# A three-branch mixer layer with a seven-product output projection: other halves of K, sums made earlier, a block-wise finish

## The reference, cut to what matters

```python
h = _rmsnorm(x, norm_g)                    # x: 1024 x 2048
proj = einsum('sd,de->se', h, w_in)        # to 5120 columns
ua, va, ga, q, k, v, gb, xc, gc = split(proj)
ya = _spatial_gating(ua, va, ...)          # mixer A, 4 tiles of 128 columns
yb = _swa_sink_attention(q, k, v, ...)     # mixer B, 8 tiles
yc = _multiscale_pool(xc, ...)             # mixer C, 4 tiles
mix = concatenate([ya * silu(ga), yb * silu(gb), yc * silu(gc)])
out = _rmsnorm(x + einsum('se,ed->sd', mix, w_out), final_g)
```

## Time and profile before

| what | value |
|---|---|
| time, median of 3 runs | 1334.62 us (1334.57 to 1339.37) |
| the profiled execution: time / span | 1337.06 us / 1335.3 us |
| TensorE matmul busy | 1277.5 us (96%) |
| VectorE / ScalarE busy | 798.5 us (60%) / 456.7 us (34%) |
| mean granted TensorE clock | 0.985 |
| DMA, mean over the span | 177 GB/s, 235.99 MB |

### The profile page before, as it was taken

How to read it: one execution, slowest core, us unless ns; L and a number is a source line. 1 busy time by engine, 2 the same in 40 slices (tenths; PEclk the granted TensorE clock), 3 DMA queues, 4 the chain that set the end, 5 groups by cost and what they waited for, 6 DMA issues and landing times. The chain is left out here.

```text
span 1335.3 us, 15960 instructions
## 1 busy us (share of the span) xinstructions
PE 1277.5 (96%) x6374; PEld 1058.6 (79%) x6374; DVE 798.5 (60%) x1157; ACT 456.7 (34%) x661; POOL 45.1 (3%) x38
## 2 busy tenths in 40 slices
PE   6999999999999998999999999999794999999995
PEld 4988888888888887888888888888673888888884
DVE  7444787767345564535786765357573665545664
ACT  6433433333232344424333333233322212223135
POOL 4200000000000212000000000000000000000000
PEclk9999999999999999999999999999898999999998
DMA  6642221212266444323121222357888689867857
GB/s 214 199 126 97 93 95 64 95 64 95 66 236 231 161 165 153 113 85 111 68 95 64 95 67 92 106 210 279 335 325 320 252 309 384 328 229 255 326 200 267
DMA packets 67514, 235.99 MB, mean 177 GB/s; under 512 B 7249, under 2 KB 10353, under 8 KB 54257
## 3 DMA queue, kind: packets, MB, share of 16 engines
q1 hardware_dynamic: 67440, 234.99, 49.4%
HBM read 192.23 MB, written 42.73 MB: 176 GB/s over the span
## 5 line engine op out<-in xcount | busy, mean ns | idle before, releaser
L1304 PE MATMUL t_bank<-op_hi,w_hi 128*128 128x512 f32 x1088 | 432.0, 397 | 22.7 <-DVE op_lo L902 10.8
L1305 PE MATMUL t_bank<-op_lo,w_hi 128*128 128x512 f32 x1088 | 426.6, 392 | 0.0
L1306 PE MATMUL t_bank<-op_hi,w_lo 128*128 128x512 f32 x1088 | 426.4, 392 | 0.0
L897 DVE TENSOR_TENSOR w_lo<-raw,w_hi 128x1024 fp32r<-128x1024 f32 (+1 forms) x172 | 203.0, 1220 | 320.4 <-ACT w_hi L678 320.4
L678 ACT ACTIVATE w_hi<-raw 128x1024 fp32r<-128x1024 f32 (+1 forms) x172 | 169.4, 1031 | 376.6 <-PE t_bank L1306 313.5
L1304 PEld LDWEIGHTS t_bank<-op_hi,w_hi 128*128 128x128 f32 x1088 | 206.0, 189 | 69.8 <-issue 14.8
L1305 PEld LDWEIGHTS t_bank<-op_lo,w_hi 128*128 128x128 f32 x1088 | 206.0, 189 | 43.0 <-issue 1.7
L1306 PEld LDWEIGHTS t_bank<-op_hi,w_lo 128*128 128x128 f32 x1088 | 205.6, 189 | 43.3
L1304 PE MATMUL n_bank<-w_hi,s_ring 128*128 128x512 f32 x448 | 176.0, 393 | 17.4 <-DVE y L986 17.4
L1306 PE MATMUL n_bank<-w_hi,s_ring 128*128 128x512 f32 x448 | 175.3, 391 | 0.0
L1305 PE MATMUL n_bank<-w_lo,s_ring 128*128 128x512 f32 x448 | 175.2, 391 | 0.0
(11 more groups left out here) (158 smaller groups left out, 1139.2 us busy)
## 6 DMA issues: line engine op xcount, KB each, us to landing
raw<-w_dram SPq DMA_DIRECT2D x78, 1024.0 KB, 4.9
s_ring<-s_parts SPq DMA_DIRECT2D x112, 512.0 KB, 5.6
s_parts<-stage SPq DMA_DIRECT2D x40, 256.0 KB, 3.1
s_parts<-stage SPq DMA_DIRECT2D x16, 512.0 KB, 3.6
raw<-w_o_dram SPq DMA_DIRECT2D x8, 1024.0 KB, 9.0
y_w<-w_o_dram SPq DMA_DIRECT2D x8, 1024.0 KB, 9.0
y<-x_dram SPq DMA_DIRECT2D x8, 1024.0 KB, 8.7
mix<-x_t_dram SPq DMA_DIRECT2D x20, 256.0 KB, 6.5
```

The lines of the kernel that those rows point to most:

```text
L897: ve.tensor_tensor(w_lo[:, J % 2, part], w_source(J)[:, part], w_hi[:, J % 2, part].bitcast(F32), ALU.subtract).then_inc(lo_done, 1)
L1304: pe.matmul(psum_out, stat[0], mov[0], start=first, stop=False)
L1305: pe.matmul(psum_out, stat[0], mov[1], start=False, stop=False)
L1306: return pe.matmul(psum_out, stat[1], mov[0], start=False, stop=last)
```

## The change

It pairs neighbouring mix tiles in the two halves of K (w_out's rows are reordered on the host to match), moves the sums, splits them in two steps a slot apart, keeps A22 in two stage slots of its own semaphore, changes the waits of load_s, swaps two residual loads, and runs the last product's add and the finish in one loop over the blocks. Cut to its core:

```diff
-SUM_ORDER = (0, 1, 2, 3) + tuple(4 + j for j in POOL_ORDER)
-SUM_AT = (70, 72, 73, 75, 76, 78, 80, 81)
-SUM_ITEMS = (Q_S3, Q_S1, Q_S2, Q_S4, Q_A22)
+K_1 = (0, 2, 4, 6, 8, 10, M_C + POOL_ORDER[0], M_C + POOL_ORDER[2])
+K_2 = (1, 3, 5, 7, 9, 11, M_C + POOL_ORDER[1], M_C + POOL_ORDER[3])
+SUM_AT = (56, 60, 64, 68, 71, 74, 77, 81)
...
             def load_first_half(r):
+                else:
+                    sp.wait_ge(s_saved[0], 32 * r)
+                    sp.wait_ge(s_saved[1], 32 * r)
+                if r == 4:
                     sp.wait_ge(o_ready, PIECES * HALVES)
...
+                sp.dma_start(a11, mix_first[K_1[r]]).then_inc(a_loaded, 16)
+                sp.dma_start(a12, mix_first[K_2[r]]).then_inc(a_loaded, 16)
...
+            def save_first_sums(r):
+                m1, m2 = sum_tiles(r)[2:4]
+                sp.wait_ge(s_lo_done, 5 * r + 1)
+                sp.dma_start(s_parts[Q_A22, r].rearrange("p h s -> p (h s)"),
+                             stage[:, 0:2, :].bitcast(F32).rearrange("p h s -> p (h s)")).then_inc(a22_saved, 16)
+                sp.wait_ge(s_lo_done, 5 * r + 2)
+                save_halves(Q_S1, r, 2, m2)
+                sp.wait_ge(s_lo_done, 5 * r + 3)
+                save_halves(Q_S3, r, 3, m1)
+            def save_last_sums(r):
+                a11, a12 = sum_tiles(r)[0:2]
+                sp.wait_ge(s_lo_done, 5 * r + 4)
+                save_halves(Q_S2, r, 0, a11)
+                sp.wait_ge(s_lo_done, 5 * r + 5)
+                save_halves(Q_S4, r, 1, a12)
+            def sums_traffic(J):
+                for r in range(8):
+                    if SUM_AT[r] + 1 == J:
+                        save_first_sums(r)
+                    if SUM_AT[r] + 2 == J:
+                        save_last_sums(r)
+                for r in range(8):
+                    if SUM_AT[r] - 1 == J:
+                        load_first_half(r)
...
             def load_s(n):
                 if n == 2 * Q_S2:
+                    sp.wait_ge(s_saved[0], 32 * 4)
+                if n == 2 * Q_S2 + 1:
                     for slot in range(4):
-                        sp.wait_ge(s_saved[slot], 32 * 10)
+                        sp.wait_ge(s_saved[slot], 32 * 8)
+                    sp.wait_ge(a22_saved, 16 * 8)
...
+                if n == 5:
+                    load_residual(0, R_22)
                 if n == 4:
-                    load_residual(0, R_22)
-                if n == 5:
                     load_residual(0, R_21)
...
+            def first_sums_hi(r):
+                m1, m2 = sum_tiles(r)[2:4]
+                tile_final(sc, o_evac, gate_used, 1, K_2[r])
...
+                    sc.wait_ge(s_saved[0], 32 * r)
+                    sc.wait_ge(s_saved[1], 32 * r)
+                sum_hi(r, 0, m2)
+                sc.wait_ge(sums_made, 4 * r + 4)
+                if r >= 1:
+                    sc.wait_ge(s_saved[2], 32 * r)
+                    sc.wait_ge(s_saved[3], 32 * r)
+                sum_hi(r, 2, m2)
+                sum_hi(r, 3, m1)
+            def last_sums_hi(r):
+                a11, a12 = sum_tiles(r)[0:2]
+                sc.wait_ge(a22_saved, 16 * (r + 1))
+                sum_hi(r, 0, a11)
+                sum_hi(r, 1, a12)
...
+            def first_sums(r):
+                a11, a12, m1, m2 = sum_tiles(r)
+                ve.wait_ge(s_hi_done, 5 * r + 1)
+                ve.tensor_tensor(stage[:, 1, :], m2, stage[:, 0, :].bitcast(F32), ALU.subtract).then_inc(s_lo_done, 1)
+                ve.wait_ge(a_loaded, 32 * (r + 1))
+                tile_final(ve, o_evac, gate_used, 1, K_1[r])
+                if r >= 1:
+                    ve.wait_ge(s_saved[2], 32 * r)
+                ve.tensor_tensor(m2, m1, m2, ALU.add).then_inc(sums_made, 1)
+                ve.wait_ge(sums_made, 4 * r + 1)
+                ve.tensor_tensor(m1, a11, m1, ALU.subtract).then_inc(sums_made, 1)
+                ve.tensor_tensor(a11, m2, a11, ALU.subtract).then_inc(sums_made, 1)
+                ve.wait_ge(sums_made, 4 * r + 3)
+                ve.tensor_tensor(a12, a12, a11, ALU.subtract).then_inc(sums_made, 1)
+                ve.wait_ge(sums_made, 4 * r + 4)
+                sum_lo(r, 1, 2, m2)
+                sum_lo(r, 2, 3, m1)
+            def last_sums(r):
+                a11, a12 = sum_tiles(r)[0:2]
+                sum_lo(r, 3, 0, a11)
+                sum_lo(r, 4, 1, a12)
...
-                    if g % 2 == 1:
+                    if g % 2 == 1 and g < CHUNKS - 1:
                         add_chain(g // 2, range(ST - 1))
...
-            add_chain(PAIRS * PRODUCTS - 1, (ST - 1,))
             for st in range(ST):
+                add_chain(PAIRS * PRODUCTS - 1, (st,))
                 finish_first(st)
```

More of the change, by code:

```diff
@@ L258, in build, with sum_tiles @@
         acc = (rstd_row[:], x_raw[:, 1, :])
-        a11 = (x_raw[:, 1, :], spare[:, 0, :])
-        a12 = (x_sq[:, 1, :], spare[:, 1, :])
-        s3 = spare[:, 2, :]
+        def sum_tiles(r):
+            first = r < 4 or r % 2 == 1
+            a11, a12 = (x_raw[:, 1, :], x_sq[:, 1, :]) if first else (spare[:, 0, :], spare[:, 1, :])
+            return a11, a12, mix[:, K_1[r], :], mix[:, K_2[r], :]
         T = [psum(f"t_bank{i}") for i in range(2)]
@@ L295, in build @@
         m_saved = [sem(f"m_saved{i}") for i in range(2)]
-        a_loaded = [sem(f"a_loaded{i}") for i in range(2)]
+        a_loaded = sem("a_loaded")
         sums_made, s_hi_done, s_lo_done = sem("sums_made"), sem("s_hi_done"), sem("s_lo_done")
         s_saved = [sem(f"s_saved{i}") for i in range(4)]
+        a22_saved = sem("a22_saved")
         s_loaded = [sem(f"s_loaded{i}") for i in range(S_SLOTS)]
@@ L538, in _ @@
                         load_x1(kt)
[L539 to L543, removed]
+                sums_traffic(J)
                 if J == IN_GROUPS - 6:
@@ L628, in copy_u @@
                     for slot in range(4):
-                        sc.wait_ge(s_saved[slot], 32 * 10)
+                        sc.wait_ge(s_saved[slot], 32 * 8)
                 else:
@@ L745, in mix_hi, with sum_hi @@
                 sc.activation(stage[:, 2 * (n % 2), :], mix[:, kt, :], ACT.Copy).then_inc(m_hi_done, 1)
-            def sums_hi(r):
-                kt, s = SUM_ORDER[r], r % 2
-                sc.wait_ge(sums_made, 4 * r + 4)
[L750 to L759, removed]
+            def sum_hi(r, slot, src):
+                sc.activation(stage[:, slot, :], src, ACT.Copy).then_inc(s_hi_done, 1)
+            def first_sums_hi(r):
+                m1, m2 = sum_tiles(r)[2:4]
+                tile_final(sc, o_evac, gate_used, 1, K_2[r])
+                if r == 0:
+                    for slot in range(2):
+                        sc.wait_ge(m_saved[slot], 32 * 8)
+                else:
+                    sc.wait_ge(s_saved[0], 32 * r)
+                    sc.wait_ge(s_saved[1], 32 * r)
+                sum_hi(r, 0, m2)
+                sc.wait_ge(sums_made, 4 * r + 4)
+                if r >= 1:
[8 more added lines that the diff above has]
+                sum_hi(r, 1, a12)
             sc.wait_ge(consts_set, 1)
@@ L865, in _ @@
                     if SUM_AT[r] == J:
-                        sums_hi(r)
+                        first_sums_hi(r)
+                    if SUM_AT[r] + 1 == J:
+                        last_sums_hi(r)
                 if half == HALVES and g // 2 % PRODUCTS == Q_A11 and g % 2 == 1:
@@ L940, in weight_sums, with sum_lo @@
+                sum_lo(r, 2, 3, m1)
+            def sum_lo(r, i, slot, tile):
+                ve.wait_ge(s_hi_done, 5 * r + i + 1)
+                ve.tensor_tensor(tile, tile, stage[:, slot, :].bitcast(F32), ALU.subtract).then_inc(s_lo_done, 1)
+            def last_sums(r):
+                a11, a12 = sum_tiles(r)[0:2]
+                sum_lo(r, 3, 0, a11)
+                sum_lo(r, 4, 1, a12)
             def weight_sums(n):
@@ L1273, in _ @@
                     if SUM_AT[r] == J:
-                        make_sums(r)
-                        sums_lo(r)
+                        first_sums(r)
+                    if SUM_AT[r] + 1 == J:
+                        last_sums(r)
                 if half == HALVES:
@@ L1529, in weight_streams @@
         parts += [tile(span(4096 + P * j, P)), tile(span(4608 + P * j, P))]
-    order = np.concatenate([pair(512, i) for i in range(8)] + [span(0, 512), span(1536, 512)])
+    tiles = [pair(512, i) for i in range(8)] + [span(a + P * j, P) for a in (0, 1536) for j in range(4)]
+    order = np.concatenate([tiles[kt] for kt in K_1 + K_2])
     blocks = w_out[order].reshape(2, 2, 4, P, PAIRS, 2, 512).transpose(4, 0, 5, 1, 3, 2, 6)
```

27 lines of the change are left out of this document (6 added, 21 removed).

## The result

The changed kernel takes 1303.11 us (median of 4 runs, 1302.34 to 1303.41), the kernel before 1335.58 us (4 runs): a ratio of 0.9751, with a 95% interval of 0.973 to 0.9772. The forecast was 1302 us, in a range of 1296 to 1315. The medians are 32.5 us apart. The span of the profiled execution went from 1335.3 to 1301.6 us, 33.7 us less, where the sum said 32.4.

What follows compares the result with a forecast made beforehand. TensorE was taken to be the bound, with 26.5 us of waits while the sums are made. Terms -31.0 + 1.0 - 2.4 = -32.4 us gave 1304.7, put at 1302 us because the median lay 2.4 lower; range 1296 to 1315.

Steps and rivals of the forecast that it cites:

- the sum: All terms together, -31.0 + 1.0 - 2.4 = -32.4 us, giving 1304.7 us against the profiled execution's 1337.06.
- Waits gone, -31.0: TensorE's waits of 17.4, 6.7 and 2.4 us between 949 and 1035 us vanish, with 4.5 us of slow clock.
- Attention at nothing: Sums placed beside attention in slots 56, 60 and 64 cost TensorE 0 us; bounds 0 and 3 x 1.0 us.
- Slots 68 to 78 at nothing: VectorE runs at most about 1 us past these 10.9 us slots, costing TensorE 0.
- Pair 7 in slot 81, 1 us in hand: The add's first block is done at 20.8 us, TensorE asks at 21.8 for slot 82; cost 0.
- The new edge, slot 84, +1.0 (0 to 6.8): copy_u of slot 83 waits for pair 7's last store, delaying TensorE at slot 84 by 1.0 us, bounds 0 and 6.8.
- The end, -2.4 (2.0 to 8.0): After the last matmuls, output stores bind and end 2.4 us earlier without their gap; bounds -2.0 and -8.0.
- Rival 1: Stores stay the edge in slots 82 to 86, two waits costing 14 us with slow clock: 1316 us; chance 0.15.
- Rival 2: Pair 7 at slot 81 is late, so the 17.4 us wait stays with its clock loss: 1321 us; chance 0.08.
- Rival 3: A22's store lands late and stops ScalarE, VectorE, then TensorE for all eight pairs: 1360 us; chance 0.02.
- Rival 4: The end is not bound by stores: up to 5.6 us better, 1297 us; chance 0.08, inside the forecast's 0.70.
- my pricing of short waits without a loss of clock: No clock fall was seen before the 2.4 us wait, so short waits were priced without slow-clock cost.

Runs made afterwards that it cites:

- e11_after_again: The changed kernel, unaltered, run again on another chip for comparison; 1302.66 us, span 1300.2 us.
- e4_slack: The changed kernel with four more VectorE operations in each of slots 56, 60 and 64; span 1305.4 us against 1301.6.
- e3_one_slot: The changed kernel with all five copies and differences of every pair in one slot instead of two; span 1319.5 us against 1301.6.
- e5_no_second_half: The changed kernel without the four 1 MB output stores of the second half of the sequence; span 1298.0 us against 1301.6.
- e9_both: The changed kernel with pair 0's residual loads later and the second half's output in sixteen 256 KB stores; 1299.77 us.
- e10_pair7: The changed kernel with only pair 7's copies and differences all in one slot; span 1315.3 us against 1301.6.
- e6_residual_later: The changed kernel with pair 0's three residual loads issued two, one and one steps later; 1302.51 us.
- e8_stores_first: The kernel before, with two 1 MB weight loads moved behind pair 6's stores in SP's list; span 1335.9 us.
- e2_tail_alone: The kernel before with only the new block-wise end; 1334.29 us against 1336.96, ratio 0.9978.
- e7_add_first: The kernel before with the first product's add ahead of pair 7's sums in slot 81; span 1323.2 us, 12.1 less.

## Why the prediction was right, point by point

- **Waits gone, -31.0.** Right in what it names, a little off in size. 26.5 us of waits went. The clock was put at 4.5 us from durations in two windows; the busy time of the page fell by 3.6, and by 5.3 to the other execution of the changed kernel (e11_after_again), so that the term cannot be judged to better than 1 us. That the measured 33.7 us are above the sum's 32.4 has one cause that no term names: the starts of the halves, outside the change, gave 1.3 us on their own.
- **Attention at nothing.** Right. The prediction had slot 57's softmax at 1.7 us late with 0.9 us of slack left. VectorE and TensorE after:

```profile
701.52 0.68 DVE L953 TENSOR_TENSOR stage<-mix,stage 128x512 fp32r<-128x512 f32 x1
...
705.63 1.29 DVE L971 TENSOR_TENSOR mix<-mix,stage 128x512 f32<-128x512 f32 x2 [0.77 <-ACT stage L768]
707.03 2.36 DVE L933 TENSOR_TENSOR w_lo<-raw,w_hi 128x1024 fp32r<-128x1024 f32 x2
...
716.21 0.69 DVE L1109 TENSOR_TENSOR probs<-probs,row_inv 128x512 f32<-128x512 f32 x1
```

```profile
717.99 0.66 PE L1467 MATMUL n_bank<-ident,probs 128*128 128x128 f32 x4
```

  The sums are done at 706.9, the softmax at 716.9, and the transposes start at 717.99: 1.1 us of slack, none waited. e4_slack bears this out: 2.86 us of added work in slot 56 cost 1.54 us of waits in slot 57 (0.61 and 0.93), so some 1.3 us were free.
- **Slots 68 to 78 at nothing.** Right for the change as written, but the argument lacked a term. I had argued these slots from VectorE's load, with stores that land in 2.9 us, and had not seen the queue behind load_s(0) and load_s(1): e3_one_slot shows pair 5's A22 store landing 10 us after its issue in slot 74. What keeps the forecast right is the split. In the changed kernel the copy that needs this store stands in slot 75, ScalarE is idle for 2.68 us before it, and TensorE does not wait.
- **Pair 7 in slot 81, 1 us in hand.** Right: VectorE begins the add at 1003.27, so the first of its blocks is done near 1003.9, and slot 82 begins at 1005.6 (21.8 us after slot 80's start, worked out below); there is no wait.

```profile
1003.27 1.88 DVE L1025 TENSOR_TENSOR y<-n_bank,y 128x512 f32<-128x512 f32 x3
```

- **The new edge, slot 84, +1.0 (0 to 6.8).** Right, at 0.7, and between 0.2 and 1.3 in the four other executions that leave this part as it is. The hand-made queue put the last store's issue at 34.7 us after slot 80's start and its landing at 44.6. By the first block of load_s(2), issued 8.7 us into slot 80, that slot starts at 983.8 here, and the last store was issued at 1018.06 and landed 9.06 later: 34.3 and 43.3.

```profile
1018.06 9.06 DMA s_parts<-x_sq
```

  At a rate of 358 GB/s, the Trainium skill's figure for the HBM share (DMA: Bandwidth & Descriptors, Bandwidth), the same count gave 3.8 us of stall. The same section gives about 358 GB/s to each core when both cores of an HBM domain stream; this kernel runs on one core. Here the measurement decides against 358 as a limit: 0.7 us of wait, 380 GB/s over the 22 us from 1000 on (window below), and 374 GB/s even for the output stores once they have no gap.

```profile
1000.00:1022.00 22.00, 22.00 (x99) 18.22 (x98) 17.74 (x17) 6.33 (x8) 0.00 (x0) 1.00 1.01 380
```

- **The end, -2.4 (2.0 to 8.0).** Right: 2.9. The cause, that stores bind it and not the chain of scaling, is shown from both sides, by e5_no_second_half (3.0 us of the end are the queue) and by e9_both (a queue that starts 2.1 us earlier against the last matmul moves the end by 2.2). The term was 0.5 low. The stores ran at 374 GB/s without the gap and at 354 to 359 before, which goes the right way, but no run separates this from the gap itself.
- **The rivals.** Rival 1 (stores stay the edge) is seen in its smallest form, 0.7 us. Rival 2 is what e3_one_slot and e10_pair7 bring about: 11.3 and 11.4 us at slot 82. Rival 3 (A22's store holds ScalarE for all pairs) did not come: the two waits of that kind, in slots 75 and 82, are 2.7 and 6.8 us in ScalarE's list, and TensorE waited for neither; behind the second, ScalarE still had 0.9 us to wait for TensorE before it could round the next weights. Rival 4 (the end not bound by stores) is refuted.
- **From the sum to the forecast.** The sum gave 1304.7 us against the profiled execution, whose time measured 1303.39; the forecast of 1302 took off 2.4 us more, because two of three runs of the kernel before lay that much lower. The later runs of the kernel before have medians of 1336.7 to 1337.7 us, so the profiled execution's 1337.06 was an ordinary one. This step was not borne out; it did no harm because its 2.4 us are of the size of the scatter.
- **Open.** Why copy_u gained 1.2 and not 2.7 us from the residual load taken away (e6_residual_later) is only in part explained. In that run the last of pair 7's stores was issued 0.8 us later (1018.90 instead of 1018.06) and landed about 1.9 us sooner after its issue. The A22 store also landed 0.8 us later, with nothing changed ahead of it; from its issue to the copy that needs it the changed kernel's two executions themselves differ by 0.6 us (8.5 and 8.0). And no run undoes the new pairing of tiles, or A22's own slots, apart from the earlier places of the sums: what each of these gives alone is not shown.

## What to carry to other kernels

When two engines wait on each other through a store, look first at what stands behind them in their lists: here the order of one add against a pair of sums was worth 9 us by itself, and the split into two steps mattered only for the two pieces of work whose store met a full queue. The stall on a queue of transfers was not removed by reordering transfers inside the same stretch (e8_stores_first); it went when bytes moved to a stretch in which the queue was nearly idle, and when nobody waited in the meantime. At the end of a kernel, count the bytes still to be written from the first store on: if they fill the time, as here, look for an earlier first store or for a gap to close.

## What the runs showed of the hardware that was not expected

Waits of TensorE of nearly the same length did different things to its clock. In the kernel before, 2.4 us of waiting for the pool mean at slot 77 left it at 1.00; in e3_one_slot, 2.5 us of the same kind at slot 75 were followed by five microseconds at 0.66, that is partly at 1.2 GHz. The windows behind the wait, before and in e3_one_slot:

```profile
972.00:977.00 5.00, 5.00 (x21) 3.80 (x21) 4.20 (x6) 0.63 (x1) 0.00 (x0) 1.00 0.78 282
```

```profile
940.00:945.00 5.00, 4.74 (x12) 3.48 (x13) 3.83 (x5) 0.63 (x1) 0.00 (x0) 0.66 0.82 287
```

The slot is not what decides, and within this range neither is the length. The wait at slot 77 is 2.2 us in e2_tail_alone and 2.5 in e7_add_first, and the clock stays at 1.00 behind both. In e8_stores_first it is the shortest of all, and the clock falls. That wait, and the window behind it:

```profile
PE e_bank L1493 <- DVE aux L1090: 1.9, 1, 1.9
```

```profile
971.00:976.00 5.00, 5.00 (x13) 3.34 (x14) 4.20 (x6) 0.78 (x2) 0.00 (x0) 0.66 0.76 270
```

So my pricing of short waits without a loss of clock was right by the row and luck in part: of five such waits of 1.9 to 2.5 us, two cost clock.

The second point is the size of the output stores. Stores of 256 KB, with 2 KB for each row, cost no bandwidth against those of 1 MB: in e9_both sixteen of them were issued in 10.2 us at the head of the queue, and from the first issue to the end the 8.39 MB took 24.4 us, against 24.5 in e11_after_again.
